# Gates and branch projections with weights 512 wide as the moving operand, merged branches transposed, weight loads held at the start

## The chip, the cores and the metric
One core of one Trainium2 chip. The metric is the device time of one execution, in microseconds (us).

## The reference
One layer of a hybrid encoder, 256 tokens by 2048 channels, float32. The parts that the change touches:

```
h = RMSNorm_pre(x)
gate_logits = (h @ W_in)[..., last 4096 columns]
g_ssm, g_attn = split(sigmoid(gate_logits + b_gate))        # 2 x (256, 2048)
merged = g_ssm * (y_ssm @ W_ssm_out) + g_attn * (y_attn @ W_attn_out)
x = x + RMSNorm_post(merged @ W_mix_out)
```

y_ssm has 4096 channels and y_attn 2048. Before this come the other columns of W_in, the state-space scan and the attention; behind it a feed-forward block (up projection, convolution, GeGLU, down projection).

## The kernel before
Every product with a weight is made in three parts, so that it is nearly exact in float32: ACT copies a weight slot to a rounded high part w_hi (`split`, L480), DVE takes raw minus w_hi as the low part w_lo (`lo`, L824), and the activations lie in SBUF as a high and a low part side by side. hi x hi, hi x lo and lo x hi are added up in PSUM. The unit of this stream is a half: 128 x 512 weights, 256 KB. SP loads raw weights in units of two halves into four slots; there are four slots of w_hi and w_lo, and ACT and DVE run up to three halves ahead of TensorE (LEAD = 3).

There are two ways to use a half on TensorE (PE). `half` (L1345) is narrow: the weights are stationary, 128 columns at a time, and the activations move, 512 columns (high and low) against w_hi and 256 columns (high) against w_lo: eight matmuls, 3072 moving columns. The output is transposed, channels on partitions, 256 tokens in columns; the low columns and the high ones lie in two halves of a bank. ACT copies one of them to `tmp` (`main_copy`, L489) and DVE adds the other (`evac`, L830). `wide_half` (L1357) is the other way: 128 tokens of activations are stationary and the weights move, 512 columns, three matmuls for each of two groups of tokens: six matmuls, 3072 moving columns. The output has tokens on partitions and needs one read of a bank.

The stages are Q and S (the projections with attention and scan beside them), G (gates, 128 halves), O (branches, 192 halves), M (mix, 64 halves), U (up, 256 halves) and D (down, 128 halves). M and D are wide, the others narrow. Each engine has its own program in order, loops (`Fori`) with the same turn structure on all engines, and semaphores: `lo_done` (w_lo is there), `half_used` (PE is done with a half), `tile_out` (an output tile has been read from its banks). G beside its products makes the grouped RMSNorm of the scan's output: squares on ACT, their sums on GpSimd, a product with ones on PE behind a turn's seventh half (L1537), scaling and splitting into y_s on DVE and ACT. In O a turn makes 256 channels of both branches: 16 halves of y_s and 8 of o_s; DVE multiplies with the gate (`gated_branch`), adds the branches (`merge`), and the sum, already transposed, is split into h_s (`merged_hi` L689, `merged_lo` L1176) for M. Behind the last turn the merge and the split come before ACT loads its Sqrt table (L735) and before M's next splits; three halves of M have been split by then.

At the start SP issues two 1 MB loads of x and then the weight loads without a wait. DVE and ACT square each half of x as it lands, x is scaled, PE transposes it (`h_bank`, L1372), ACT and DVE split it into h_s, and the first halves go in between.

Of the kernel before, what the change touches and what calls it, by code (L numbers as in the profile page):

```python
# [24 lines left out]
F32 = mybir.dt.float32  # L25
# [39 lines left out]
for _name, _n in (("mix_pre", 16), ("ffn_pre", 16), ("gate_b", 32), ("xbc_b", 48), ("ssm_norm", 32),  # L65
                  ("ffn_b", 64), ("xbc_w", 192), ("ffn_w", 192)):
    PAR[_name] = _at
    _at += _n
# [7 lines left out]
for _name, _halves, _tiles in (("Q", 136, 34), ("S", 320, 80), ("G", 128, 32), ("O", 192, 32), ("M", 64, 8),  # L76
                               ("U", 256, 64), ("D", 128, 8)):
    HALF[_name], TILE[_name] = _h, _t
    _h += _halves
    _t += _tiles  # L80
HALVES = _h
LEAD = 3
# [4 lines left out]
PAR_LOADS = 12  # L87
# [32 lines left out]
def build(nc, x, norm_mix_pre, norm_mix_post, norm_ffn_pre, norm_ffn_post, w_in, b_gate, conv_xbc_w,  # L120
# [3 lines left out]
    with ctx:  # L124
# [9 lines left out]
        def place(name, shape, dt, at):  # L134
# [11 lines left out]
        w_lo, at = place("w_lo", [P, 4, 2, 256], F32R, at)  # L146
        tmp, at = place("tmp", [P, 2, T], F32, at)
# [6 lines left out]
        mt_b, _ = place("mt_b", [P, 2, 3 * P], F32, at)  # L154
        sq, at = place("sq", [P, 2, T], F32, at)
# [11 lines left out]
        gate, _ = place("gate", [P, 32, T], F32, RG)  # L167
# [90 lines left out]
        yn_done, yn_hi, y_split, gate_tanh, m_split = (sem(n) for n in (  # L258
            "yn_done", "yn_hi", "y_split", "gate_tanh", "m_split"))
# [30 lines left out]
        def _(sp):  # L290
# [37 lines left out]

            for m in range(4):
                plain(win, m, V0, m, m)  # L330
# [52 lines left out]
        def _(pool):  # L383
# [19 lines left out]
            rows = {"mix_pre": norm_mix_pre, "ffn_pre": norm_ffn_pre, "gate_b": b_gate, "xbc_b": conv_xbc_b,  # L403
# [54 lines left out]
            with pool.Fori(0, GROUPS) as i:  # L458
                for n in range(3):
# [15 lines left out]
        def _(act):  # L475
# [188 lines left out]
            with act.Fori(0, GROUPS) as i:  # L664
                for j in range(16):
# [23 lines left out]
            def merged_hi(i):  # L689

                for t in range(2):
                    act.wait_ge(yn_done, i * 2 + (33 + t))
                    dst = h_s[:, 2 * i + t, 0:T] if isinstance(i, int) else (
                        h_s[:, bass.ds(i * 2 + t, 1), 0:T].rearrange("p a t -> p (a t)"))
                    act.activation(dst, yn[:, t, :], ACT.Copy, scale=0.5).then_inc(yn_hi, 1)

            def branch_turn(i, before):
                for j in range(24):
                    split(i, 24, H + j + LEAD)
                    if before is not None and j == 3:  # L700
                        merged_hi(before)
                    if j in (2, 4, 6, 8):
                        g = i * 2 + ((j - 2) // 4 * 16 + (j - 2) // 2 % 2)
                        act.activation(tile_of(gate, g), tile_of(gate, g), ACT.Tanh, scale=0.5,
                                       bias=col("gate_b", g)).then_inc(gate_tanh, 1)
                    if j in (15, 23):
                        for t in range(2):
                            n = 2 * (j // 16) + t
                            main_copy(i, 24, 4, H + j, N + n, n)

            branch_turn(0, None)
            with act.Fori(1, 8) as i:
                branch_turn(i, i - 1)
            merged_hi(7)
# [909 lines left out]
```

## Time and profile before

| | us |
|---|---|
| median of 3 runs (lowest, highest) | 1855.43 (1854.22, 1856.04) |
| profiled execution | 1854.61 |
| its span, first to last instruction | 1852.8 |
| PE busy | 1809.3 (98%) |
| DVE busy | 1310.1 (71%) |
| ACT busy | 1113.7 (60%) |
| GpSimd busy | 95.5 (5%) |
| HBM read | 340.05 MB, with writes 185 GB/s |

The granted clock of TensorE is 0.993 as a mean. A busy PE is not PE at its peak: matmuls overlap, so the distance between starts tells the pace, not the duration of one. LDWEIGHTS (PEld) is the load of the stationary operand and overlaps the matmul before it.

### The profile page before, as it was taken

Reading aid. Unit: us, or ns where it says so; the run is one execution under the profiler, and the core shown is the slowest. Engines: PE = TensorE matmul, PEld = TensorE weight load, DVE = VectorE, ACT = ScalarE, POOL = GpSimd, SP = SyncE. Lnnn points to the kernel's source line nnn. Section 1 sums busy time; section 2 is a strip of 40 time slices with the busy share of each in tenths; the row PEclk is TensorE's granted clock in tenths of the full one; section 3 lists DMA queues with packets and bytes.
Section 4 is the critical chain, followed back from the end, with each engine's and each line's share of the span. In section 5 each row is a group of like instructions: output and inputs, shape, how many; then the busy total and the mean of one; then the engine's idle time right before and its main releaser. Section 6 shows DMA issues by size and latency. Waiting matters only on the chain.

```text
span 1852.8 us, 36223 instructions
## 1 busy us (share of the span) xinstructions
PE 1809.3 (98%) x10131; PEld 1556.3 (84%) x10131; DVE 1310.1 (71%) x2510; ACT 1113.7 (60%) x2223; POOL 95.5 (5%) x154
## 2 busy tenths in 40 slices
PE   7999999999999999999999999997999999999997
PEld 6888888888888888888888888886888888887886
DVE  5766688888888888777756655655677777775554
ACT  6554566666666666777655555545666666664443
POOL 2000001110010110111100000000000000000000
PEclk9999999999999999999999999999999999999999
DMA  7656656765666665566655555665466666665664
GB/s 205 201 163 189 181 178 176 204 188 166 201 188 181 175 203 168 172 183 186 185 190 179 188 190 183 205 225 183 137 191 183 192 191 192 185 181 182 193 196 144
DMA packets 402986, 342.80 MB, mean 185 GB/s; under 512 B 28960, under 2 KB 373168, under 8 KB 402432
## 3 DMA queue, kind: packets, MB, share of 16 engines
q1 hardware_dynamic: 398240, 325.14, 58.7%
q0 software_dynamic: 4672, 17.15, 2.8%
q8 instruction: 20, 0.33, 0.1%
q14 instruction: 22, 0.18, 0.0%
q10 hardware_dynamic: 32, 0.01, 0.0%
HBM read 340.05 MB, written 2.16 MB: 185 GB/s over the span
## 4 chain that ended last, share of the span: by engine, by line
PE 92%; DVE 3%; ACT 2%; issue 2%; DMA 0%; DVEq 0%; ACTq 0%; SPq 0%
PE bank L1351 49%; PE bank L1353 25%; PE bank L1364 14%; PE bank L1369 3%; ACT w_hi L487 1%; DVE cc L1016 1%; DMA x_rows<-in_x 0%; PE bank L1483 0%; DVE xc L1027 0%; ACT mix_junk L749 0%; DVE w_lo L827 0%; DVE out_t L1339 0%; DVE upad L833 0%; ACT cc L597 0%; PE bank L1383 0%
## 5 line engine op out<-in xcount | busy, mean ns | idle before, releaser
L827 DVE TENSOR_TENSOR w_lo<-raw,w_hi 128x512 fp32r<-128x512 f32 x1224 | 844.5, 697 | 447.6 <-ACT w_hi L487 433.1
L487 ACT ACTIVATE w_hi<-raw 128x512 fp32r<-128x512 f32 x1224 | 756.6, 628 | 444.6 <-PE bank L1353 318.8
L1351 PE MATMUL bank<-h_s,w_hi 128*128 128x512 f32 x2336 | 840.2, 403 | 0.4 <-DVE h_s L845 0.3
L1353 PE MATMUL bank<-h_s,w_lo 128*128 128x256 f32 x2336 | 655.2, 280 | 0.0
L1351 PEld LDWEIGHTS bank<-h_s,w_hi 128*128 128x128 f32 x2336 | 439.2, 188 | 108.7 <-issue 4.6
L1351 PE MATMUL bank<-o_s,w_hi 128*128 128x512 f32 x1280 | 446.8, 393 | 0.0
L1353 PEld LDWEIGHTS bank<-h_s,w_lo 128*128 128x128 f32 x2336 | 441.8, 189 | 0.6
L1353 PE MATMUL bank<-o_s,w_lo 128*128 128x256 f32 x1280 | 358.6, 280 | 0.0
L1351 PEld LDWEIGHTS bank<-o_s,w_hi 128*128 128x128 f32 x1280 | 239.7, 187 | 53.8
L1353 PEld LDWEIGHTS bank<-o_s,w_lo 128*128 128x128 f32 x1280 | 241.9, 189 | 0.0
L1351 PE MATMUL bank<-y_s,w_hi 128*128 128x512 f32 x512 | 181.2, 399 | 0.0
L1364 PE MATMUL bank<-w_hi,y_s 128*128 128x512 f32 x512 | 159.2, 392 | 3.1 <-DVE w_lo L827 3.1
L1353 PE MATMUL bank<-y_s,w_lo 128*128 128x256 f32 x512 | 143.8, 281 | 0.0
L494 ACT ACTIVATE tmp<-bank 128x256 f32<-128x256 f32 x242 | 79.7, 382 | 101.1 <-PE bank L1353 101.1
L1364 PEld LDWEIGHTS bank<-w_hi,y_s 128*128 128x128 f32 x512 | 96.8, 189 | 23.7 <-DVE w_lo L827 3.5
L1351 PEld LDWEIGHTS bank<-y_s,w_hi 128*128 128x128 f32 x512 | 96.2, 188 | 24.1
L1364 PE MATMUL bank<-w_lo,y_s 128*128 128x512 f32 x256 | 100.3, 392 | 0.0
L1353 PEld LDWEIGHTS bank<-y_s,w_lo 128*128 128x128 f32 x512 | 96.7, 189 | 0.0
L1364 PE MATMUL bank<-w_hi,h_s 128*128 128x512 f32 x256 | 80.5, 394 | 2.1 <-DVE w_lo L827 2.1
L1364 PEld LDWEIGHTS bank<-w_hi,h_s 128*128 128x128 f32 x256 | 48.9, 191 | 12.9 <-DVE w_lo L827 2.6
L1016 DVE SCALAR_TENSOR_TENSOR cc<-upad,par,cc 128x256 f32<-128x256 f32 x144 | 59.0, 479 | 0.0
L1364 PEld LDWEIGHTS bank<-w_lo,y_s 128*128 128x128 f32 x256 | 48.5, 189 | 10.1
(205 smaller groups left out, 1191.4 us busy)
## 6 DMA issues: line engine op xcount, KB each, us to landing
raw<-in_w_in SPq DMA_DIRECT2D x576, 256.0 KB, 3.0
raw<-in_w_up SPq DMA_DIRECT2D x256, 256.0 KB, 3.2
raw<-in_w_ssm_out SPq DMA_DIRECT2D x128, 256.0 KB, 2.9
raw<-in_w_down SPq DMA_DIRECT2D x128, 256.0 KB, 3.4
raw<-in_w_attn_out SPq DMA_DIRECT2D x64, 256.0 KB, 2.9
raw<-in_w_mix_out SPq DMA_DIRECT2D x64, 256.0 KB, 3.6
cs_rows<-cs_dram POOLq DMA_DIRECT2D x16, 512.0 KB, 4.9
cs_rows<-cs_dram POOLq DMA_DIRECT2D x16, 256.0 KB, 6.2
```

What stands on the lines that cost most here:

```text
L487: act.activation(w_hi[:, c % 4, :, :], raw[:, slot, 2 * m:2 * m + 2, :], ACT.Copy).then_inc(hi_done, 1)
L494: act.activation(tmp[:, n % 2, :], bank[b][:, 0:T], ACT.Copy).then_inc(main_out, 1)
L827: dve.tensor_tensor(w_lo[:, c % 4, :, :], raw[:, (c // 2) % 4, 2 * (c % 2):2 * (c % 2) + 2, :], w_hi[:, c % 4, :, :].bitcast(F32), ALU.sub ...
L1016: ins = dve.scalar_tensor_tensor(out=cc[:, t, :], in0=upad[:, t, n:n + T], scalar=col("xbc_w", tile[t] + n * 48), in1=cc[:, t, :], op0=ALU ...
L1351: pe.matmul(bank[b][:], w_hi[:, w[0], w[1], w[2]], src[:, k0 + k, :], start=start and k == 0, stop=False, skip_group_check=True)
L1353: last = pe.matmul(bank[b][:, T:2 * T], w_lo[:, w[0], w[1], w[2]], src[:, k0 + k, 0:T], start=False, stop=True, skip_group_check=True)
L1364: last = pe.matmul(bank[b + t][:], src[:, kt, at + P * t:at + P * t + P], w, start=kt == 0 and w is hi and at == 0, stop=True, skip_group_ ...
L1369: return pe.matmul(o, a, b, start=start, stop=True, skip_group_check=True)
```

## The change
G and O use `wide_half`. In G a turn makes 1024 gate columns in two groups of sixteen halves; the gates lie with tokens on partitions, and DVE adds the bias, which GpSimd loads for each 512 columns and spreads to all partitions (`gate_out`); ACT's copies and the bias in ACT's tanh are gone. In O there are four turns of 48 halves instead of eight of 24; DVE multiplies straight from the bank, 512 columns by 128 tokens at a time, and adds the branches into a new tile `both`. The sum now has tokens on partitions, so PE transposes it, eight 128 x 128 transposes for each 512 channels (`merged_t`), behind the sixth half of the next turn, the last ones behind M's third half; ACT and DVE split the result from PSUM, likewise later in the turn. ACT waits for all gates before its first tanh. SP's loads for G and O are `wide`: rows of 2 KB instead of 1 KB. At the start SP waits for the first half of x before the first weight load, and PE makes six products of ones and the identity once x's second half is there. `UNCOPIED` only shifts counts.

```diff
@@ sync
+            sp.wait_ge(x_in[0], 16)
             for m in range(4):
                 plain(win, m, V0, m, m)
...
-            with sp.Fori(0, 16) as i:
-                for m in range(4):
-                    plain(win, m, i * 256 + GATE0, i * 4 + (u + m), m)
+            with sp.Fori(0, GROUPS) as i:
+                for m in range(8):
+                    wide(win, m, i * WIDE + GATE0, i * 8 + (u + m), m % 4)
             u = HALF["O"] // 2
-            with sp.Fori(0, 8) as i:
+            with sp.Fori(0, 4) as i:
+                for m in range(16):
+                    wide(wssm, m, i * WIDE, i * 24 + (u + m), m % 4)
                 for m in range(8):
-                    plain(wssm, m, i * 256, i * 12 + (u + m), m % 4)
-                for m in range(4):
-                    plain(wattn, m, i * 256, i * 12 + (u + 8 + m), m)
+                    wide(wattn, m, i * WIDE, i * 24 + (u + 16 + m), m % 4)
@@ gpsimd, G
             with pool.Fori(0, GROUPS) as i:
+                pool.wait_ge(tile_out, i * 2 + TILE["G"])
+                pool.dma_start(gate_bias[:], b_gate[:, bass.ds(i * WIDE, WIDE)].rearrange("a c -> (a c)")
+                               .partition_broadcast(P)).then_inc(bias_in, 16)
@@ scalar, G, O and M
-                    if j % 8 == 7:
-                        for t in range(2):
-                            k = j // 8
-                            main_copy(i, 16, 4, H + j, N + 2 * k + t, 2 * k + t)
...
+            def merged_hi(c):
+                for n in range(4):
+                    kt = c * 4 + n
+                    act.wait_ge(m_mm, c * 4 + (n + 1))
...
+                    act.activation(dst, bank[4 + n][:, 0:T], ACT.Copy, scale=0.5).then_inc(m_hi, 1)
             def branch_turn(i, before):
-                for j in range(24):
-                    split(i, 24, H + j + LEAD)
-                    if before is not None and j == 3:
+                for j in range(48):
+                    split(i, 48, H + j + LEAD)
+                    if before is not None and j == 7:
                         merged_hi(before)
                     if j in (2, 4, 6, 8):
...
+                        at = gate[:, t, bass.ds(i * WIDE + D * b, WIDE)]
+                        act.activation(at, at, ACT.Tanh, scale=0.5).then_inc(gate_tanh, 1)
+            act.wait_ge(tile_out, N)
...
+            def mix_turn(i, first):
                 for k in range(2):
                     for j in range(16):
                         split(i, 32, H + 16 * k + j + LEAD)
+                        if first and (k, j) == (0, 1):
+                            merged_hi(3)
@@ vector, G and O
+            def gate_out(i, k):
+                dve.wait_ge(half_used, i * 32 + (H + 16 * k + 16))
+                dve.wait_ge(bias_in, i * 32 + (16 * k + 16))
+                for t in range(2):
+                    dve.tensor_tensor(gate[:, t, bass.ds(i * (2 * WIDE) + WIDE * k, WIDE)], bank[2 * k + t][:], gate_bias[:],
+                                      ALU.add).then_inc(tile_out, 1)
...
             def gated_branch(i, b):
+                dve.wait_ge(half_used, i * 48 + (H + 32 + 16 * b))
                 for t in range(2):
+                    g = gate[:, t, bass.ds(i * WIDE + D * b, WIDE)]
+                    dve.wait_ge(gate_tanh, i * 4 + (2 * b + t + 1))
+                    dve.scalar_tensor_tensor(out=g, in0=g, scalar=1.0, in1=bank[2 * b + t][:], op0=ALU.add,
+                                             op1=ALU.mult).then_inc(tile_out, 1)
             def merge(i):
                 for t in range(2):
+                    dve.wait_ge(tile_out, i * 4 + (N + 3 + t))
+                    dve.tensor_tensor(both[:, t, :], gate[:, t, bass.ds(i * WIDE, WIDE)],
+                                      gate[:, t, bass.ds(i * WIDE + D, WIDE)], ALU.add).then_inc(merged, 1)
+            def merged_lo(c):
+                for n in range(4):
...
+                    dve.wait_ge(m_hi, c * 4 + (n + 1))
+                    dve.scalar_tensor_tensor(out=part(T), in0=bank[4 + n][:, 0:T], scalar=0.5, in1=part(0).bitcast(F32),
+                                             op0=ALU.mult, op1=ALU.subtract).then_inc(m_split, 1)
+            def branch_turn(i, before):
+                for j in range(48):
+                    lo(i, 48, H + j + LEAD)
+                    if before is not None and j == 7:
+                        merged_lo(before)
+                    if j in (31, 47):
+                        gated_branch(i, j // 47)
+                merge(i)
@@ tensor
+            pe.wait_ge(x_in[1], 16)
+            for n in range(6):
+                mm(bank[3][:, 0:P], ones[:], ident[:])
             for kt in range(4):
                 h_bank(kt)
...
+                    for j in range(16):
+                        wide_half(i, 32, H + 16 * k + j, h_s, j, 2 * k)
+                        if j == 6:
+                            pe.wait_ge(sq_added, i * 6 + (3 * k + 3))
+                            pe.wait_ge(misc_read, i * 2 + (MISC_G + k))
+                            mm(misc[:, 0:T], ones[:], sq_sum[:]).then_inc(misc_ready, 1)
...
+            def merged_t(c):
+                pe.wait_ge(merged, c * 2 + 2)
+                for n in range(4):
+                    for t in range(2):
+                        last = pe.transpose(bank[4 + n][:, P * t:P * t + P], both[:, t, P * n:P * n + P], ident[:])
+                    last.then_inc(m_mm, 1)
+            def branch_turn(i, before):
+                pe.wait_ge(tile_out, i * 4 + (N - 2))
+                for j in range(32):
+                    pe.wait_ge(y_split, j + 1)
+                    wide_half(i, 48, H + j, y_s, j, 0)
+                    if before is not None and j == 5:
+                        merged_t(before)
+                pe.wait_ge(tile_out, i * 4 + N)
+                for j in range(16):
+                    wide_half(i, 48, H + 32 + j, o_s, j, 2)
...
+            def mix_turn(i, first):
                 for k in range(2):
                     pe.wait_ge(tile_out, i * 4 + (N + 2 * k - 2))
                     for j in range(16):
-                        if k == 0:
+                        if first and k == 0:
                             pe.wait_ge(m_split, j + 1)
                         wide_half(i, 32, H + 16 * k + j, h_s, j, 2 * k)
+                        if first and (k, j) == (0, 2):
+                            merged_t(3)
```

## Rows read from the trace of the kernel before

**Rows 1.** The page: busy time of an engine; the chain that ended last.

```profile
PE 1809.3 (98%) x10131; PEld 1556.3 (84%) x10131; DVE 1310.1 (71%) x2510; ACT 1113.7 (60%) x2223; POOL 95.5 (5%) x154
...
PE 92%; DVE 3%; ACT 2%; issue 2%; DMA 0%; DVEq 0%; ACTq 0%; SPq 0%
```

**Rows 2.** In order of time, PE, end of O and M: start, duration, [idle before].

```profile
1190.02 0.40 PE L1351 MATMUL bank<-o_s,w_hi 128*128 128x512 f32 x1
...
1194.62 0.40 PE L1351 MATMUL bank<-o_s,w_hi 128*128 128x512 f32 x1
...
1194.97 0.40 PE L1364 MATMUL bank<-w_hi,h_s 128*128 128x512 f32 x1
...
1196.13 0.62 PE L1364 MATMUL bank<-w_hi,h_s 128*128 128x512 f32 x2
...
1198.17 0.62 PE L1364 MATMUL bank<-w_hi,h_s 128*128 128x512 f32 x2
...
1201.38 0.50 PE L1364 MATMUL bank<-w_hi,h_s 128*128 128x512 f32 x1 [2.15 <-DVE w_lo L827]
```

**Rows 3.** Busy time by stretch; the sixth entry is the granted clock.

```profile
1202.00:1206.00 4.00, 4.00 (x12) 3.13 (x11) 1.83 (x3) 0.80 (x2) 0.00 (x0) 0.57 1.01 417
```

**Rows 4.** In order of time, PE, the first turn of G.

```profile
745.18 0.50 PE L1351 MATMUL bank<-h_s,w_hi 128*128 128x512 f32 x1 [0.15 <-DVE w_lo L827]
...
750.72 0.28 PE L1353 MATMUL bank<-h_s,w_lo 128*128 128x256 f32 x1
...
751.50 0.28 PE L1353 MATMUL bank<-h_s,w_lo 128*128 128x256 f32 x1
```

**Rows 5.** In order of time, PE: first product of O, last of M.

```profile
923.61 0.40 PE L1351 MATMUL bank<-y_s,w_hi 128*128 128x512 f32 x1
...
1285.89 0.39 PE L1364 MATMUL bank<-w_hi,h_s 128*128 128x512 f32 x1
```

**Rows 6.** In order of time, PE, the start of D.

```profile
1662.34 0.62 PE L1364 MATMUL bank<-w_hi,y_s 128*128 128x512 f32 x2
...
1665.78 0.39 PE L1364 MATMUL bank<-w_hi,y_s 128*128 128x512 f32 x1
```

**Rows 7.** In order of time, PE: low products around four transposes at the start.

```profile
19.95 0.28 PE L1353 MATMUL bank<-h_s,w_lo 128*128 128x256 f32 x1
...
20.73 0.28 PE L1353 MATMUL bank<-h_s,w_lo 128*128 128x256 f32 x1
```

**Rows 8.** Groups of instructions: busy us, mean ns of one, idle before.

```profile
L827 DVE TENSOR_TENSOR w_lo<-raw,w_hi 128x512 fp32r<-128x512 f32 x1224 | 844.5, 697 | 447.6 <-ACT w_hi L487 433.1
...
L487 ACT ACTIVATE w_hi<-raw 128x512 fp32r<-128x512 f32 x1224 | 756.6, 628 | 444.6 <-PE bank L1353 318.8 <-PE bank L1364 120.4 <-DMA raw<-in_w_mix_out 3.1
...
L1223 DVE TENSOR_TENSOR gained<-bank,mix_gain 128x512 f32 x8 | 5.5, 692 | 4.5 <-ACT mix_junk L726 4.0
```

**Rows 9.** In order of time: a bank of M is handed over.

```profile
1220.84 0.39 PE L1364 MATMUL bank<-w_hi,h_s 128*128 128x512 f32 x1
...
1221.19 0.60 ACT L726 ACTIVATE mix_junk<-bank 128x512 f32<-128x512 f32 x1 [0.89 <-PE bank L1364]
```

**Rows 10.** In order of time, the start.

```profile
10.62 1.23 DVE L853 CUSTOM_DVE_ANT_0 junk<-x_rows 128x1024 f32<-128x1024 f32 x1 [1.38 <-DMA x_rows<-in_x]
...
13.43 1.97 PE L1383 MATMUL bank<-ident,x_rows 128*128 128x128 f32 x8 [9.70 <-ACT x_rows L500]
...
15.66 0.80 PE L1351 MATMUL bank<-h_s,w_hi 128*128 128x512 f32 x1 [0.26 <-DVE h_s L845]
...
18.57 0.49 PE L1351 MATMUL bank<-h_s,w_hi 128*128 128x512 f32 x1
```

**Rows 11.** Busy time by stretch, the start; the last entry is GB/s.

```profile
0.00:10.00 10.00, 0.26 (x1) 0.18 (x1) 1.23 (x2) 2.70 (x5) 1.85 (x12) 1.00 0.78 241
...
8.00:10.00 2.00, 0.00 (x0) 0.00 (x0) 1.23 (x2) 1.22 (x3) 0.00 (x0) 1.00 1.02 394
10.00:12.00 2.00, 0.00 (x0) 0.00 (x0) 1.30 (x3) 1.15 (x2) 0.00 (x0) 1.00 1.10 360
```

More of the change, by code:

```diff
@@ L154, in build @@
         mt_b, _ = place("mt_b", [P, 2, 3 * P], F32, at)
+        both, _ = place("both", [P, 2, WIDE], F32, at)
         sq, at = place("sq", [P, 2, T], F32, at)
@@ L166, in build @@
         out_t, _ = place("out_t", [P, 2, D], F32, RO)
-        gate, _ = place("gate", [P, 32, T], F32, RG)
+        gate, _ = place("gate", [P, 2, 2 * D], F32, RG)
         gained, _ = place("gained", [P, 2, D], F32, RG)
@@ L697, in branch_turn @@
             def branch_turn(i, before):
-                for j in range(24):
-                    split(i, 24, H + j + LEAD)
-                    if before is not None and j == 3:
+                for j in range(48):
+                    split(i, 48, H + j + LEAD)
+                    if before is not None and j == 7:
                         merged_hi(before)
                     if j in (2, 4, 6, 8):
[L703 to L709, printed above, removed]
+                        t, b = (j // 2 - 1) % 2, (j - 2) // 4
+                        at = gate[:, t, bass.ds(i * WIDE + D * b, WIDE)]
+                        act.activation(at, at, ACT.Tanh, scale=0.5).then_inc(gate_tanh, 1)
@@ L1238, in _ @@
                         lo(i, 32, H + 16 * k + j + LEAD)
-                    if k == 0:
+                        if first and (k, j) == (0, 1):
+                            merged_lo(3)
+                    if first and k == 0:
                         dve.wait_ge(gain_in[0], 16)
                     wide_gain(i, 4, N + 2 * k, 2 * k, mix_gain, k)
-            inverse(0, lambda: dve.wait_ge(main_out, N + 8))
+            mix_turn(0, True)
+            with dve.Fori(1, 2) as i:
+                mix_turn(i, False)
+            inverse(0, lambda: dve.wait_ge(main_out, N - UNCOPIED + 8))
             dve.wait_ge(x_again_in, 32)
@@ L1531, in _ @@
             H, N = HALF["G"], TILE["G"]
[L1532 to L1555 removed]
+            with pe.Fori(0, GROUPS // 2) as i:
                 for k in range(2):
@@ L1558, in _, with mix_turn @@
                     for j in range(16):
-                        if k == 0:
+                        wide_half(i, 32, H + 16 * k + j, h_s, j, 2 * k)
[3 more added lines that the diff above has]
+                            mm(misc[:, 0:T], ones[:], sq_sum[:]).then_inc(misc_ready, 1)
+            H, N = HALF["O"], TILE["O"]
+            def merged_t(c):
[14 more added lines that the diff above has]
+                    wide_half(i, 48, H + 32 + j, o_s, j, 2)
+            branch_turn(0, None)
+            with pe.Fori(1, 4) as i:
+                branch_turn(i, i - 1)
+            H, N = HALF["M"], TILE["M"]
+            def mix_turn(i, first):
+                for k in range(2):
+                    pe.wait_ge(tile_out, i * 4 + (N + 2 * k - 2))
+                    for j in range(16):
+                        if first and k == 0:
                             pe.wait_ge(m_split, j + 1)
                         wide_half(i, 32, H + 16 * k + j, h_s, j, 2 * k)
+                        if first and (k, j) == (0, 2):
+                            merged_t(3)
+            mix_turn(0, True)
+            with pe.Fori(1, 2) as i:
+                mix_turn(i, False)
             def h2_bank(kt):
```

149 lines of the change are left out of this document (46 added, 103 removed).

## The prediction
> **What bounds the kernel now.** I read the page's busy shares and its chain of waits first, then TensorE in order of time at the edges of the stages the change touches. TensorE (PE) is busy 98% of the span and holds 92% of the chain [rows 1]; ACT and DVE have room. So time is what the PE stream costs per half (one slot of split weights, 3072 moving columns either way), plus what the PE loses at stage edges and at the start. The reader is to see three things.
>
> First, the pace. A narrow half is four pairs of 512 and 256 columns. Late in the branch stage, 13 pairs take 1194.62 - 1190.02 = 4.60 us, 0.354 a pair, 1.41 us a half. A wide half is two triples of 512 columns: three triples take 1198.17 - 1196.13 = 2.04 us, 0.680 a triple, 1.36 us a half [rows 2]. The columns are equal (1.28 us at 2.4 GHz); what differs is the eight instructions against six.
>
> Second, one edge: entering the mix stage the PE stands 2.15 us for a w_lo [rows 2], and right behind it four microseconds have a mean clock of 0.57, so PE is at 1.2 GHz most of that time: 4 x 0.43 = 1.7 us more [rows 3].
>
> Third, the start: the PE's first transpose is at 13.43, 2.81 us after the second half of x lets DVE go at 10.62 [rows 10].
>
> **Gates (128 halves).** Seven halves precede the row-sum product. Halves 3 to 6 start at 745.18, after a stall of 0.31 (0.15 of it shown as idle), and three halves at 1.41 lie before it, so the stage starts at 745.18 - 0.31 - 4.23 = 740.64 [rows 4]. The branch stage starts at 923.61 [rows 5]: 182.97 us. The row-sum product of ones moves the low product from 750.72 to 751.50, 0.78 where a pair takes 0.35: 0.43 us, eight times 3.44 [rows 4]. That and the 0.31 stay. After: 128 x 1.36 + 3.44 + 0.31 = 177.8. **Saved 5.1.**
>
> The PSUM traffic changes hands: ACT's copies go, DVE adds a bias to two 512-wide banks per sixteen halves, 0.69 us each [rows 8]. PE uses the other pair of banks for the next 16 halves (22 us), so this costs nothing. DVE's burst of 1.5 us delays the next w_lo; PE has three halves (4.08 us) in hand. On GpSimd the bias DMA and its wait (the last tile's eviction) come before the row-sum adds; they start about 2.5 us later in a group, and their product is wanted only after seven halves, 9.5 us: hidden. SP issues as many transfers of the same size. At the end ACT waits for DVE's last bias additions, with its splits behind it: 0.35 + 1.5 us, then split 0.63 and w_lo 0.70 [rows 8, 9] gives 3.2 of the 4.08 us: hidden, 0.9 us in hand, and lost one for one beyond.
>
> **Branches (192 halves).** Before: 1194.97 - 923.61 = 271.36 us [rows 2, 5], 1.413 a half throughout. After: 192 x 1.36 = 261.1. Added: eight transposes per chunk, three chunks here. Four of the start's transposes move the low product by 20.73 - 19.95 - 0.35 = 0.43 us [rows 7], so eight take 0.85: 2.55 in all. PE's new y_split waits are met long before. The end of each turn is the tight place. DVE gets the bank about 0.35 us after the next half has begun (1220.84 against 1221.19, where ACT is the reader [rows 9]); two gate products and two merges of 512 columns at 0.69 with a 0.06 gap make 3.0 (fused products are not shown at this width; as bounds I take the 0.69 and 0.70 of the plain ones, 0.75 if their scalar form costs more); then w_lo 0.70. That is 4.05 against 4.08 us of PE work. The weight load of that half wants to go first, so I take 0.2 us of stall at each of three turns (0 to 0.5): 0.6. At the gate products of the first branch the burst is only 1.5 us: nothing. ACT's four tanh of a turn, 512 wide, and its four halved copies (about 1.6 us in a row) come when it has seven or more halves before the next edge; it needs 0.63 of 1.36 us: hidden. After: 264.3. **Saved 7.1.**
>
> **Mix.** Before: from 1194.97 to 1285.89 + 0.23 = 1286.12 [rows 2, 5], 91.15 us, which is 64 x 1.36 = 87.04 and 4.1 of loss (stall 2.4, clock 1.7). The stall was DVE's and ACT's last merge, then the Sqrt table, then split and w_lo, one after the other. After, ACT loads the table and goes on splitting; the merge's copies wait until the transposes behind the third half. What is late next is w_lo of half 3 (the same 4.05 against 4.08: 0.2) and, behind four copies and four splits, w_lo of half 5 (0.15). Transposes 0.85. The 3 MB that GpSimd asks for at this edge now meet a PE that is 4 us ahead; weights of halves 10 and 11 are issued 3 us earlier too, so I take nothing, with 2 us as the bad bound. After: 88.2. **Saved 2.9** (0 to 3.8).
>
> **Start.** Weights wait for the first half of x. By 10.6 us the queues moved 2.41 MB + 0.6 x 0.36 = 2.6 MB, of which x is 2.1: half a megabyte of weights went between, 1.3 us at 0.39 MB/us [rows 11]. I take 1.2 (0 to 1.4). Held weights are issued at about 7 to 8 us and the first slot, at most 1 MB with what is left of x, takes 2.6 us; it is wanted past 12: hidden. Below nothing it could go only by that slot being late, at most 1 us. The six added products lie in the 2.8 us between x's landing and the first transpose: by the 0.43 us of a 256-column product at full clock, 128 columns at half clock cost 0.43, six 2.6. Then first half and four transposes, 18.57 - 15.66 = 2.91 us before [rows 10], take 1.41 + 0.43 if the clock is up: 1.07 less, of which I take 0.7, since the second half also waits for h. **Saved 1.9** (-1 to 2.4).
>
> On that clock: before, PE began with transposes at 13.43 and ordinary products at 15.66, and rows behind 18 have full-clock durations [rows 10]. The Trainium skill ("TensorE: Matmul & The Clock Gate", Part 4: PE-mode transpose) says that transposes do not count as PE activity for the clock. By that rule the added products are the only activity before the first half, and the 0.7 may be absent, since PE then only transposes for 2 us; the trace cannot separate the two readings.
>
> **Sum.** 5.1 + 7.1 + 2.9 + 1.9 = 17.0 us off the profiled execution's 1854.61 us (its span 1852.8 and 1.8 around it): 1837.6. The median of the runs shown is 1855.43, 0.8 above it; I forecast 1838.0.
>
> **Rivals.**
> (a) Wide halves in these stages run as at the start of the down projection: 1665.78 - 1662.34 = 3.44 us for five triples, 0.688 [rows 6], 1.376 a half. 320 x 0.016 = 5.1 back; and with nothing from the start, 1.9 more. 1843 to 1845. For: narrow halves pace differently by stage too. Against: mix holds 0.680.
> (b) The gain per half is not there: only columns count, and the fewer instructions bring nothing. Then the transposes (2.55) and turn stalls (0.6) stand against mix and start (4.8): 1.65 us saved, 1853. Against: 1.41 and 1.36 stand on the two sides of one edge, 2 us apart [rows 2]. The Trainium skill ("TensorE: Matmul & The Clock Gate", Back-to-back issue gap) puts the gap of a full-clock matmul at N/2.4 + 2.5 ns. By it a narrow half is 1.300 and a wide one 1.295, an estimate of 320 x 0.005 = 1.6 us in all, so 1851.7 here. The rows have 0.227 for 512 columns, 13 ns above the columns, not 2.5; the measurement decides.
> (c) Slower: the handover in the branches. If DVE's burst at the eight handovers of that stage, from the bank's release to w_lo, is 2.1 us longer than 4.05, PE stalls as at the old mix edge, and the clock drops each time: 4.1 x 8 = 33 us, 1870. It turns the sign when each costs more than 2.1 us. For: the margin at the four turn ends is nil. Against: the mid-turn handovers have 1.5 us of slack, and the durations are well known.
> (d) Better: no turn stalls, the full start gain and 3.8 at mix: 1835 or a little less.
>
> **How the numbers follow.** Forecast and its neighbourhood with (d), 1833 to 1841: 0.70. (a), 1841 to 1846: 0.18. Between (a) and (b): 0.05. (b): 0.03. (c): 0.04. The range, 1832 to 1846, holds the first two and leaves out under 2 in 10. A measurement of this kernel tells 0.2%, 3.7 us, from no change, so faster is all but (b) and (c): 0.93; same is (b), 0.03; slower (c), 0.04.
>
> **What would show it.** The wide products of the gate and branch stages at 0.680 a triple, about 178 and 264 us between the first products of the stages; no idle PE at the mix edge and a clock of 1.0 there; turn ends with at most 0.3 us of idle before a wide product, released by w_lo; eight transposes in 0.85 us; DVE's first look at x's second half near 9.4 and the first half's products at full-clock durations from its first pair. Wrong would be: 0.688 or more a triple, idle of 1 us or more at turn ends, ACT waiting for raw weights at the start or past the mix edge, or products of 0.43 us spacing there.

## The result and the profile after

| | us |
|---|---|
| changed kernel, median of 6 runs | 1846.39 (1839.73 to 1849.49) |
| kernel before beside it, 6 runs | 1855.74 (1854.22 to 1861.21) |
| ratio | 0.9939, 95% interval 0.9921 to 0.9956 |
| profiled execution of the changed kernel: its span | 1844.3 |

The forecast was 1838.0 with a range of 1832 to 1846: faster as forecast, but by 9.3 us instead of 17.4, and the median is 0.4 above the upper end of the range. The page answers to [rows 1]:

```profile
PE 1804.5 (98%) x9535; PEld 1529.3 (83%) x9535; DVE 1288.5 (70%) x2437; ACT 1096.2 (59%) x2143; POOL 99.8 (5%) x161
...
PE 91%; DVE 3%; ACT 2%; issue 2%; DMA 1%; DVEq 0%; ACTq 0%; SPq 0%
```

PE still sets the time. It has some 600 instructions fewer, as eight products a half became six in 320 halves (640 fewer), while 32 transposes and the six products (two rows each) were added: 10131 - 9535 = 596. Its busy time fell by only 4.8. So the stages have to be read one by one. Their edges are the first products of G, O and M, the last of M, and the first of D (start, duration):

```profile
740.41 0.40 PE L1371 MATMUL bank<-w_hi,h_s 128*128 128x512 f32 x1
...
919.01 0.39 PE L1371 MATMUL bank<-w_hi,y_s 128*128 128x512 f32 x1
...
1182.85 0.39 PE L1371 MATMUL bank<-w_hi,h_s 128*128 128x512 f32 x1
...
1272.24 0.39 PE L1371 MATMUL bank<-w_hi,h_s 128*128 128x512 f32 x1
...
1655.11 0.40 PE L1371 MATMUL bank<-w_hi,y_s 128*128 128x512 f32 x1
```

The same edges, taken in the profile of every kernel that is told of below, in us. "To G" is the time from the start of the span. G of "before" and of e10 begins at the point worked out as in the prediction, G of e2 and e5 at the 512th product with w_hi ahead of O. "M to U" is the gap between M's last product and the first of U's opening; D ends with its last product, and about 11.7 us follow it in every profile.

| profile | to G | G | O | M | M to U | U | D | span |
|---|---|---|---|---|---|---|---|---|
| before | 740.64 | 182.97 | 271.36 | 91.15 | 11.83 | 363.93 | 179.13 | 1852.8 |
| after | 740.41 | 178.60 | 263.84 | 89.62 | 11.46 | **371.18** | 177.51 | 1844.3 |
| e1, after again | 739.77 | 178.58 | 263.84 | 90.60 | 11.46 | 363.71 | 179.11 | 1838.7 |
| e5, before again | 741.55 | 182.84 | 266.23 | 91.14 | 11.84 | 371.72 | 180.17 | 1857.2 |
| e2, narrow G and O | 740.24 | 183.16 | 271.26 | 90.01 | 11.46 | 363.79 | 179.10 | 1850.8 |
| e3, no hold | 740.14 | 178.62 | 263.84 | 92.48 | 11.45 | 363.99 | 179.11 | 1841.3 |
| e4, no six products | 741.67 | 178.57 | 263.84 | 93.68 | 11.45 | 363.75 | 179.08 | 1843.7 |
| e6, late x | 740.28 | 178.57 | 263.84 | 87.95 | 11.45 | 363.78 | 179.11 | 1836.7 |
| e7, products in U | 740.59 | 178.58 | 263.84 | 90.57 | 11.45 | 374.36 | 180.32 | 1851.4 |
| e8, other order | 734.64 | 178.57 | 263.84 | 92.12 | 11.46 | 365.47 | 180.25 | 1838.1 |
| e9, other order, late x | 734.58 | 178.57 | 263.84 | 87.95 | 11.46 | 366.83 | 179.11 | 1834.0 |
| e10, before in the other order | 735.87 | 182.28 | 267.52 | 91.17 | 11.83 | 365.62 | 180.29 | 1846.2 |

The first two lines say where the gain went. G gave 4.37, O 7.52, M 1.53, D 1.62 (behind D's opening stall of 3.1 us the products kept their full pace; in every other profile some of them run at half pace, so this is luck and no part of the change), the start 0.23, the gap before U 0.37: 15.6 us. U, whose code is the same in both kernels, took 7.25 back, and 15.6 - 7.25 = 8.4 is what the spans differ by, within 0.1.

What PE waited for in the changed kernel (total us, times, longest):

```profile
PE bank L1376 <- DVE diag L1259: 11.3, 1, 11.3
PE bank L1376 <- DMA x_rows<-in_x: 6.7, 1, 6.7
PE bank L1371 <- DVE w_lo L835: 4.7, 3, 3.1
PE bank L1395 <- DMA mix_rows<-in_norm_mix_pre: 3.6, 1, 3.6
PE bank L1493 <- DVE o_s L1013: 1.1, 7, 0.2
PE bank L1358 <- DVE h_s L853: 0.3, 1, 0.3
```

Only three waits are for w_lo: 3.1 where D begins, 1.40 in M, and 0.25 in G's third half, the one that [rows 4] have. None of the handovers of a bank in G and O stalls, neither at turn ends nor inside them. In O, the chunk's eight transposes between two wide products, in order of time:

```profile
992.22 0.39 PE L1371 MATMUL bank<-w_hi,y_s 128*128 128x512 f32 x1
992.46 1.03 PE L1560 MATMUL bank<-ident,both 128*128 128x128 f32 x8
993.25 0.48 PE L1371 MATMUL bank<-w_hi,y_s 128*128 128x512 f32 x1
993.56 0.39 PE L1371 MATMUL bank<-w_lo,y_s 128*128 128x512 f32 x1
...
994.25 0.40 PE L1371 MATMUL bank<-w_lo,y_s 128*128 128x512 f32 x1
...
994.94 0.39 PE L1371 MATMUL bank<-w_lo,y_s 128*128 128x512 f32 x1
...
995.62 0.39 PE L1371 MATMUL bank<-w_lo,y_s 128*128 128x512 f32 x1
```

The transposes hold the next product back by 993.25 - 992.46 = 0.79, and the one behind it comes after 0.31 instead of 0.227, 0.09 more. Read the low products behind them: 0.69, 0.69, 0.68 apart. Whatever is put between wide products leaves the next few triples 0.01 longer; then they are at 0.680 again.

The edge into M, which answers to [rows 2, 3], on ACT, DVE, GpSimd (POOL) and PE:

```profile
1182.34 1.28 ACT L736 ACT_TABLE_LOAD   x1
...
1183.25 1.28 DVE L1183 SCALAR_TENSOR_TENSOR gate<-gate,bank 128x512 f32 x2 [0.20 <-PE bank L1371]
1183.31 1.07 POOL L476 DMA_DIRECT2D x_again<-in_x  x2 [280.29 <-PE bank L1371]
...
1184.45 1.29 DVE L1189 TENSOR_TENSOR both<-gate 128x512 f32 x2
...
1197.42 1.15 ACT L495 ACTIVATE w_hi<-raw 128x512 fp32r<-128x512 f32 x2 [4.67 <-DMA raw<-in_w_mix_out]
...
1198.92 0.47 PE L1371 MATMUL bank<-w_hi,h_s 128*128 128x512 f32 x1 [1.40 <-DVE w_lo L835]
```

The old stall of 2.15 is gone: ACT has the table at 1183.6 and goes on splitting. DVE's burst lasts from 1183.25 to 1184.45 + 1.29 = 1185.74, 2.49 us and not the 3.0 of the forecast, since two products of 512 columns take 1.28 and not 1.44. But some 15 us into M a new stall stands: ACT has no raw weights for 4.67 us, and PE runs dry for 1.40. Two megabytes of x, asked for by GpSimd at 1183.31, are the suspect; e6 below moves them. Windows of after, then of e6, in which the two loads of x come later (the third figure from the end is the granted clock, then DMA share and GB/s):

```profile
1190.00:1195.00 5.00, 5.00 (x24) 4.14 (x23) 2.39 (x4) 1.38 (x3) 0.00 (x0) 1.00 0.96 340
```

```profile
1190.00:1195.00 5.00, 5.00 (x24) 4.14 (x23) 2.92 (x5) 2.23 (x4) 0.00 (x0) 1.00 0.79 247
```

At the start, against [rows 10]:

```profile
10.61 1.23 DVE L861 CUSTOM_DVE_ANT_0 junk<-x_rows 128x1024 f32<-128x1024 f32 x1 [1.38 <-DMA x_rows<-in_x]
10.63 2.93 PE L1376 MATMUL bank<-ident,ones 128*128 128x128 f32 x12 [6.73 <-DMA x_rows<-in_x]
...
13.42 1.97 PE L1390 MATMUL bank<-ident,x_rows 128*128 128x128 f32 x8
15.65 0.50 PE L1358 MATMUL bank<-h_s,w_hi 128*128 128x512 f32 x1 [0.26 <-DVE h_s L853]
...
17.84 0.50 PE L1358 MATMUL bank<-h_s,w_hi 128*128 128x512 f32 x1
```

(The six products appear as x12, two rows each.) The second half of x comes at 10.61 where it came at 10.62: the hold brought nothing. The first half of the stream begins at the same 15.65, but its first product takes 0.50 and not 0.80, and the second half begins at 17.84 where it began at 18.57: 0.73 less.

The U stage: low products of after, fifteen pairs from the first row to the last:

```profile
1399.88 0.28 PE L1360 MATMUL bank<-o_s,w_lo 128*128 128x256 f32 x1
...
1405.18 0.28 PE L1360 MATMUL bank<-o_s,w_lo 128*128 128x256 f32 x1
```

and of e1, the same kernel run again:

```profile
1399.97 0.28 PE L1360 MATMUL bank<-o_s,w_lo 128*128 128x256 f32 x1
...
1405.17 0.28 PE L1360 MATMUL bank<-o_s,w_lo 128*128 128x256 f32 x1
```

5.30 / 15 = 0.3533 a pair against 5.20 / 15 = 0.3467. U has 1024 pairs, and 1024 x 0.0067 = 6.8 us of the 7.5 between the two profiles. The narrow stream has two paces.

### The profile page after: what moved, and what is told of

The parts are those of the page before. It is cut to its first block, busy times and chain, and to the rows that moved or that the text cites. A ratio compares the mean times of both kernels' runs of the same rounds, so it can differ in the third digit from the quotient of the medians.

```text
span 1844.3 us, 34324 instructions
## 1 busy us (share of the span) xinstructions
PE 1804.5 (98%) x9535; PEld 1529.3 (83%) x9535; DVE 1288.5 (70%) x2437; ACT 1096.2 (59%) x2143; POOL 99.8 (5%) x161
## 4 chain that ended last, share of the span: by engine, by line
PE 91%; DVE 3%; ACT 2%; issue 2%; DMA 1%; DVEq 0%; ACTq 0%; SPq 0%
PE bank L1371 37%; PE bank L1358 33%; PE bank L1360 17%; PE bank L1376 3%; ACT w_hi L495 1%; DVE cc L1024 1%; DMA raw<-in_w_mix_out 1%; DMA x_rows<-in_x 0%; PE bank L1493 0%; DVE w_lo L835 0%; DVE xc L1035 0%; ACT mix_junk L757 0%; DVE upad L841 0%; DVE out_t L1346 0%; ACT cc L605 0%
## 5 line engine op out<-in xcount | busy, mean ns | idle before, releaser
L1358 PE MATMUL bank<-h_s,w_hi 128*128 128x512 f32 x1824 | 658.4, 403 | 0.4 <-DVE h_s L853 0.3
L1360 PE MATMUL bank<-h_s,w_lo 128*128 128x256 f32 x1824 | 512.0, 281 | 0.0
L1358 PEld LDWEIGHTS bank<-h_s,w_hi 128*128 128x128 f32 x1824 | 342.6, 188 | 85.9 <-issue 4.7
L1360 PEld LDWEIGHTS bank<-h_s,w_lo 128*128 128x128 f32 x1824 | 344.8, 189 | 0.4
L1371 PE MATMUL bank<-w_hi,y_s 128*128 128x512 f32 x1024 | 317.0, 389 | 3.1 <-DVE w_lo L835 3.1
L1371 PE MATMUL bank<-w_hi,h_s 128*128 128x512 f32 x768 | 240.8, 392 | 1.7 <-DVE w_lo L835 1.7
L1371 PEld LDWEIGHTS bank<-w_hi,y_s 128*128 128x128 f32 x1024 | 192.2, 188 | 43.4 <-DVE w_lo L835 3.5
L1371 PE MATMUL bank<-w_lo,y_s 128*128 128x512 f32 x512 | 199.2, 389 | 0.0
L1371 PEld LDWEIGHTS bank<-w_hi,h_s 128*128 128x128 f32 x768 | 144.1, 188 | 32.5 <-issue 1.8
L1371 PE MATMUL bank<-w_lo,h_s 128*128 128x512 f32 x384 | 149.4, 389 | 0.0
```

The lines of the kernel that those rows point to most:

```text
L1358: pe.matmul(bank[b][:], w_hi[:, w[0], w[1], w[2]], src[:, k0 + k, :], start=start and k == 0, stop=False, skip_group_check=True)
L1360: last = pe.matmul(bank[b][:, T:2 * T], w_lo[:, w[0], w[1], w[2]], src[:, k0 + k, 0:T], start=False, stop=True, skip_group_check=True)
L1371: last = pe.matmul(bank[b + t][:], src[:, kt, at + P * t:at + P * t + P], w, start=kt == 0 and w is hi and at == 0, stop=True, skip_group_ ...
```

## The experiments

**e1: the changed kernel, unchanged.** No edit; it asks what the program's own runs do.

> The changed kernel as it is, to see how the same program varies. In the profile of the change the up projection, whose code is unchanged, runs at 0.353 us per narrow pair from its second turn to its end (371.2 us from first product to the down projection's first); before it ran at 0.347 (363.9 us). Theory A: a stream of narrow pairs is locked in one of two paces and keeps it until something else is put in between, which pace it gets is chance, and this is what hides 7 us of the gain. Then single runs spread over about 7 to 10 us (1839 to 1850), and this profile's up projection takes either 364 or 371 us, with the profiled time following: about 1839 to 1841 with 364, 1846 to 1848 with 371. Theory B: the change itself slows the up projection (data placement, what is left in flight). Then it is at 0.353 in every profile of a kernel with the change, and the spread of the runs has another place.

Measured: 1842.91 us (median of 12, 1840.4 to 1851.44), the kernel before beside it 1850.16 (18 runs, 1847.45 to 1857.34), ratio 0.9966 (0.9949 to 0.9983). The times lie in groups: seven between 1840.4 and 1843.2, five between 1846.7 and 1851.5. Those of before do too: twelve at 1847.5 to 1850.4, six at 1855.6 to 1857.4. One program therefore has steps of about 7 us in it, as large as the effect that was to be measured: beside this set the change is worth 7.3 us, beside the first one 9.3. The table shows what one such step is: U at 363.71 in place of 371.18; G and O agree within 0.02. Even its faster group is 2 to 5 us above the forecast of 1838.

**e5: the kernel before, once more, profiled.**

> The kernel before once more, for its stages in a second profile. Theory A (paces by chance): its branch stage, 271.36 us at 0.353 a pair in the first profile, takes 266.3 or 271.4 us, the gates again alternate between 0.347 and 0.353 from turn to turn, and the up projection takes about 364 or 371 us; the runs of the kernel before fall in groups some 7 us apart accordingly (1848 to 1850 and 1856 to 1857 beside the last set). If the branch stage is 266.3 here, the change's gain in it is 2.5 us and not 7.5. Theory B (paces belong to the code): the same three numbers as in the first profile, 271.4 and 363.9.

Measured: 1859.21. Its O takes 266.23 where it took 271.36, its U 371.72 where it took 363.93. The low products of its O, fifteen pairs:

```profile
999.85 0.28 PE L1353 MATMUL bank<-y_s,w_lo 128*128 128x256 f32 x1
...
1005.05 0.27 PE L1353 MATMUL bank<-y_s,w_lo 128*128 128x256 f32 x1
```

0.3467, where [rows 2] have 0.354. So the 1.41 us a half on which the forecast rests is not a property of the narrow form, but one of its two paces. G again has both: from one row-sum product to the next its pace is 0.353, twice 0.347, then 0.353 and 0.347 by turns.

**e2: G and O narrow again, all else as changed.**

```diff
-                        wide_half(i, 32, H + 16 * k + j, h_s, j, 2 * k)
+                        half(i, 32, H + 16 * k + j, h_s, 2 * (j % 8), 2 * k, 2 * k + 1, j == 0)
...
-                    wide_half(i, 48, H + j, y_s, j, 0)
+                    half(i, 48, H + j, y_s, 2 * (j % 16), 0, 1, j == 0)
...
-                    wide_half(i, 48, H + 32 + j, o_s, j, 2)
+                    half(i, 48, H + 32 + j, o_s, 2 * (j % 8), 2, 3, j == 0)
```

One line more is changed: O's first half waits for all of y_s at once, and the other halves no longer wait for it.

> The changed kernel with TensorE's products in the gate and branch stages narrow again (weights stationary, 512 and 256 moving columns), all else as changed: loads, bias additions, gate products, transposes, edges. The sums in the banks then are not the reference's; only the time counts. Theory A (the gain in the two stages is the pace of the stream, 1.36 us a half against 1.387 or 1.413): the 320 halves take 320 x 0.027 to 0.053 = 8.6 to 17 us more, 1855 to 1863 us by the median, and the two stages show 0.347 or 0.353 a pair. Theory C (the gain comes from what stands around the products, ACT's copies and the edges, and the stream's form is worth 0.005 a half): within 2 us of the change.

Measured: 1860.25 (7 runs, 1852.44 to 1862.85), ratio to before 1.0041 (1.002 to 1.0062), where the changed kernel beside it had 0.9966. All else that was changed, taken together (the transposes, DVE's and ACT's new work, the start), does not make the kernel faster; the gain hangs on the wide products. The profiled execution is the fastest of the seven: its span is 1850.8 against e1's 1838.7, 12.1 more, of which G has 4.6 and O 7.4 (271.26 against 263.84), with U alike (363.79, 363.71). In its G the pace switches at each row-sum product, 0.3467 and 0.3533 by turns, as it does in the kernel before from its second one on. In its O it switches at each of the three groups of transposes, so O here is half at either pace.

**e7: a product of ones inside each of U's turns.** From its second turn on U has nothing between its narrow products that could switch the pace; here one product is put in.

```diff
                         half(i, 16, H + 8 * k + j, o_s, 2 * j, 2 * k, 2 * k + 1, j == 0)
+                        if not first and (k, j) == (0, 6):
+                            mm(misc[:, 0:T], ones[:], par[:, 0:T])
```

> The changed kernel with one product of ones and 256 columns of constants, as in the gates stage before, put into each turn of the up projection behind its seventh half; its result is not used. In the gates stage before, the pace changed at each such product and held in between. Theory A (the pace is a locked state that an inserted product switches): the up projection shows 0.347 and 0.353 in turn, takes (364 + 371)/2 + 15 x 0.43 = 374 us whatever the start, and the runs lie close together, near 1849. Theory H (the pace belongs to the turn's data or to the time of the other engines): one pace throughout, 370 or 377 us, and the spread of 7 us stays.

Measured: U 374.36, kernel 1851.86 (12 runs, 1848.96 to 1853.74). Low products of two turns that follow each other, eleven pairs each:

```profile
1327.47 0.28 PE L1360 MATMUL bank<-o_s,w_lo 128*128 128x256 f32 x1
...
1331.29 0.28 PE L1360 MATMUL bank<-o_s,w_lo 128*128 128x256 f32 x1
...
1350.10 0.28 PE L1360 MATMUL bank<-o_s,w_lo 128*128 128x256 f32 x1
...
1353.99 0.28 PE L1360 MATMUL bank<-o_s,w_lo 128*128 128x256 f32 x1
```

3.82 / 11 = 0.347, then 3.89 / 11 = 0.354, and from there each stretch is at the other pace than the one before it. Of the fifteen products put in, the first left the pace as it was and the other fourteen each switched it; between two of them it never changed. The spread is 4.8 us instead of 11, as one expects when each execution has both paces in U in about equal parts. So the pace holds until something comes between. That U's pace is what divides e1's groups fits the two profiles at hand (U 371.18 at 1845.96 us, 363.71 at 1840.40); the other runs have no profile.

**e8: another order in the narrow form.** High, high, low, low instead of high, low, high, low.

```diff
                     for t, b in enumerate((b0, b1)):
                         pe.matmul(bank[b][:], w_hi[...], src[:, k0 + k, :], ...)
+                    for t, b in enumerate((b0, b1)):
                         last = pe.matmul(bank[b][:, T:2 * T], w_lo[...], src[:, k0 + k, 0:T], ...)
```

> The changed kernel with the products of every narrow half in another order: for each of the two rows of weights first both 512-column products, then both 256-column ones (instead of 512, 256, 512, 256). The work and the sums are the same. Theory J (the two paces come from the phase of the stream as a whole): 0.347 and 0.353 as averages per pair remain, and the median is within 1 us of the change.

Measured: 1839.81 (6 runs, 1836.88 to 1840.32), ratio 0.992 (0.9896 to 0.9944). U's low products now come in pairs; two pairs apart:

```profile
1399.95 0.39 PE L1360 MATMUL bank<-o_s,w_lo 128*128 128x256 f32 x2
...
1404.83 0.40 PE L1360 MATMUL bank<-o_s,w_lo 128*128 128x256 f32 x2
```

seven times two pairs in 4.88, 0.349 a pair; over 800 pairs of U it is 0.3483, between the two old paces, and the same in e9 and e10. U takes 365.47, near the fast one. So the two paces belong to the order of the products, and not to the stream whatever its order (theory J); whether the weight load is the reason, as theory I has it, no run shows. The time up to G is 5.8 us less than in after and 5.1 less than in e1: the narrow stream of Q and S has two paces as well, and in after its stretches are at the slow one about five times as often as at the fast one. The spread is 3.4 us.

**e10: the kernel before with e8's order**, so that change and no change can be compared without the two paces.

> The kernel before with its narrow products in the order high, high, low, low, and nothing else: all its narrow stages then run at one pace, as those of the changed kernel with the same order do (1839.8). Theory (the change is worth about 5 us at like pace: G 320 pairs... worked out as 128 and 192 halves of 1.39 us against 1.36 plus eight transposes per chunk, start 0.7, M 1 us worse): about 1844.5 here, G near 181.5 and O near 267. Rival 1 (the whole gain of the change was the pace that the narrow stream happened to take): 1840 or less, the same as the changed kernel with this order. Rival 2 (the change is worth the 9 us that were measured, whatever the order): 1849.

Measured: 1847.51 (12 runs, 1844.18 to 1849.02); e8 is 1839.81, and the profiled spans are 8.2 apart. The two ran on different chips, but e9, on e10's chip, has e8's 178.57 for G and 263.84 for O, so the stages can be compared. That is nearer to the second rival (1849) than to the 1844.5 of the theory, which had G at 181.5 (182.28 measured), O at 267 (267.52) and M 1 us worse (0.95). It missed most in G (0.8), in O and at the start (0.5 each). The rival that the gain was all pace (1840) is out. Stage by stage e10 minus e8: 1.23 + 3.71 + 3.68 - 0.95 + 0.37 + 0.15 + 0.04 = 8.2 us (to G, G, O, M, the gap, U, D). M is where the changed kernel loses, although e10 keeps the old stall:

```profile
1192.10 0.50 PE L1364 MATMUL bank<-w_hi,h_s 128*128 128x512 f32 x1 [2.16 <-DVE w_lo L827]
```

**e6: x_again later.** The two loads of x wait for halves 14 and 32 of M.

```diff
-            for s in range(2):
-                pool.dma_start(x_again[:, s, :], x_view[:, s, :]).then_inc(x_again_in, 16)
             pool.dma_start(mix_gain[:], ...)
+            for s in range(2):
+                pool.wait_ge(half_used, HALF["M"] + 14 + 18 * s)
+                pool.dma_start(x_again[:, s, :], x_view[:, s, :]).then_inc(x_again_in, 16)
```

> The changed kernel with GpSimd's two loads of x for the residual (2 MB) put behind half 14 and half 32 of the mix stage, and only the 1 MB of gains at its start. Theory F (3 MB asked for at the mix edge make the weights of halves 10 and 11 late, now that the edge itself does not stall: ACT waited 4.9 to 7.1 us for raw weights and the PE 1.4 to 3.9, and the clock fell behind the longer ones): the mix stage takes 88 us instead of 89.6 to 93.7, ACT's wait for raw goes, and the median falls by 2 to 4 us. Theory G (the wait is the order of SyncE's own loads behind the late w_lo of halves 3 to 5): the PE still stands 1 us or more at about half 10.

Measured: 1838.75 (6 runs, 1838.37 to 1844.68), ratio 0.9931 (0.9905 to 0.9957). M is 87.95, which is 64 x 1.36 = 87.04 and the 0.9 of the transposes: no stall is left, and the gap before U is unchanged. The window shown above has 247 GB/s and ACT busy 2.23 us, where after had 340 and 1.38. So the loads of x held up the weights; the 1 MB of gains, still asked for at the edge, did not. The loads of x cost M 1.7 to 5.7 us in the other profiles of the changed kernel, a different amount each time; where the stall was longest (e4), it was 3.8 us and the clock fell behind it, 0.81 as a mean from 1198 to 1207.

**e3: without the hold at the start.**

```diff
-            sp.wait_ge(x_in[0], 16)
```

> The changed kernel with SyncE's wait for x's first half taken out ahead of the weight loads. Theory D (the hold brings nothing: the second half of x landed at 10.6 us before as after, since its bytes go ahead of the weights on the same queue): DVE's look at the second half stays at 10.6 us, and the first product at 15.65. Theory E (weights take bandwidth from x, and something else kept the second half late in the changed kernel): it moves later by 0.5 us or more, to above 11.1.

Measured: 1843.0 in the one run. The second half of x:

```profile
10.63 1.22 DVE L860 CUSTOM_DVE_ANT_0 junk<-x_rows 128x1024 f32<-128x1024 f32 x1 [1.40 <-DMA x_rows<-in_x]
```

10.63 with the weights free, 10.61 with them held. The weights are issued on the same SP queue behind x. From 8 to 10 us 394 GB/s are moved here and 324 with the hold, and x lands at the same time: what the weights moved, x did not lose. It is one run of each, but before and after say the same.

**e4: without the six products** (and their wait).

```diff
-            pe.wait_ge(x_in[1], 16)
-            for n in range(6):
-                mm(bank[3][:, 0:P], ones[:], ident[:])
```

> The changed kernel with the six products of ones and their wait taken out. If they bring TensorE's clock up earlier: the first half's products run at 1.2 GHz again (its first pair apart by 0.6 us instead of 0.33), and the second half starts at 18.57 instead of 17.84 us, 0.7 later. If the clock rises by the transposes alone, or the hold did it: 17.84 stays.

Measured: 1845.36 in the one run. The first products of the stream and the first of the second half:

```profile
13.31 1.97 PE L1390 MATMUL bank<-ident,x_rows 128*128 128x128 f32 x8 [9.28 <-ACT x_rows L508]
15.54 0.80 PE L1358 MATMUL bank<-h_s,w_hi 128*128 128x512 f32 x1 [0.26 <-DVE h_s L853]
...
16.34 0.63 PE L1358 MATMUL bank<-h_s,w_hi 128*128 128x512 f32 x1
...
16.99 0.63 PE L1358 MATMUL bank<-h_s,w_hi 128*128 128x512 f32 x1
...
18.97 0.54 PE L1358 MATMUL bank<-h_s,w_hi 128*128 128x512 f32 x1
```

A pair takes 0.65 up to 18, as before the change. That is the pace of half clock: e9 has 0.64 a pair at the beginning of U, at a granted clock of 0.50. (The row of the granted clock itself says 1.00 here, from 15.50 to 18.20; at the start it does not show what the products do.) The second half begins 1.13 later than in after, and G 1.26 later. The six products do bring the full pace forward. Transposes that began at 13.31 had not brought it by 15.54; products that began at 10.63 had, by 15.65. That agrees with the Trainium skill ("TensorE: Matmul & The Clock Gate", Part 4: PE-mode transpose), which says that a transpose does not count as PE-busy in the same way. The reservation is that the products also began 2.7 us earlier, and this is one run. What the prediction feared from that rule, that the gain of 0.7 would be absent, did not happen.

**e9: e8 and e6 together.**

> The changed kernel with both edits at once: narrow products in the order high, high, low, low, and the reload of x delayed to M's turns. If the two act on different stages they add: the order alone gave 1839.8 with M at 92.1 us; the delay brings M to 88.0, so 1839.8 - 4.1 = 1835.7, with the start to G at 734.6, U at 365.5 and a spread of 2 us or less outside of single runs, since the narrow stream then has one pace. Rival: the delayed transfers of x fall on U's start, where the narrow stream now takes weights at the same rate as before, and M to U grows from 11.5 by 1 to 3 us: 1837 to 1839.

Measured: 1835.36 (6 runs, 1832.69 to 1835.7), ratio 0.9886 (0.9862 to 0.9909). The two add up as expected, 1835.7. The gap before U is the same 11.46; the rival has no case. U is 1.4 longer than in e8, 1.2 of it in its first eight products: 2.70 us at a granted clock of 0.50, where e8's take 1.48; why the clock came up later is open. This is the fastest version, faster than both kernels.

## Why the prediction came out as it did

- **G, 5.1 saved: 4.4 in the profiles, size off by 0.8.** A triple has its 0.680, and no wait appeared; G is 178.6, not 177.8. G has 4.5 us over its 128 x 1.36 where 3.75 was taken: 0.44 for each of eight row-sum products (0.43 taken), 0.5 for the stall in the third half (0.31 taken), and 0.5 in steps of a hundredth, as shown behind the transposes.
- **O, 7.1 saved: 7.5 against the profile of before, 2.4 against the same kernel's other profile (266.23).** The wide side was right: 263.84 for 264.3. O has 2.72 over 192 x 1.36, so a group of transposes costs 0.9 for the assumed 0.85. The stall at turn ends did not come; DVE's burst is 2.5 and not 3.0, which leaves half a microsecond where none was.
- **M, 2.9 saved: 1.5, 0.6 in e1.** The old stall went as forecast, and with it the fall of the clock. The step that failed is the one on the 3 MB that GpSimd asks for at this edge, "so I take nothing, with 2 us as the bad bound": it cost 1.7 in after and 2.7 in e1 (M less e6's 87.95), and more in others. e6 shows the cause; with x out of the way M is 87.95, as good as the 88.2 of the forecast.
- **Start, 1.9: 0.7.** The clock term was right (0.73). The term of the hold, 1.2, was wrong: half a megabyte of weights had moved beside x, but x was none the later for it. I had read a rate as if all of it were x's to have; e3 shows that it was not. At G the start is 0.2 ahead in after and 0.9 in e1; the two paces of the stream in Q and S stand between, so these two figures do not measure the start.
- **The covers** (bias on GpSimd, DVE's additions, ACT's tanh, y_split, weights at the start) all held: the list of PE's waits has none of them.
- **The step that failed most is one that I did not write down**: that code that is not changed keeps its time. U gave 7.25 us back in the profiled execution, on a pace that changes by chance from one execution to another. [Rows 2] showed 0.354, and rival (a) even says that narrow halves "pace differently by stage too"; I took it as against the wide form and did not ask what would happen if a stage came out at its other pace. The trace of before had O at 0.353 and U at 0.347: 5.1 us of O's cost hung on one pace, and 7.5 us of U's on the other.
- **The rivals.** (a) 0.688 in place of 0.680: no, only for a few triples behind something interposed. (b) No gain per half: no, 3.7 us in G and 3.7 in O even against the middle pace. The gap of N/2.4 + 2.5 ns, which the Trainium skill gives for an isolated full-clock matmul ("TensorE: Matmul & The Clock Gate", Back-to-back issue gap), does not hold for this stream, a case that the prediction did not tell apart: 13 ns over the columns for 512 (0.680 / 3 = 0.2267 against 0.2133), and (346.7 - 320) / 2 = 13 for the products of the fast narrow pair. (c) Slower handovers: none stalled. (d) Better: of its three parts only the missing stall at turn ends came.

The like-paced comparison, e10 against e8, gives the change 7.7 us in the medians and 8.2 in the spans; the two comparisons of the kernels as they are gave 9.3 and 7.3. From the forecast's 17.0 to 8.2, by those two profiles: the narrow side was taken from an execution in which it was slow (O 271.36 for 267.52, G 182.97 for 182.28), 4.5; M at 92.12 for 88.2, and the old M there 0.02 longer, 3.9; the start 1.23 for 1.9, 0.7; the wide side of G 0.8 worse and that of O 0.5 better; the gap before U and the rest gave 0.6. 17.0 - 4.5 - 3.9 - 0.7 - 0.8 + 0.5 + 0.6 = 8.2. The mechanism was right; the sizes of the narrow side, of M and of the start were not, and how near the median came to the range is in part luck. The upper end of the range asks for 1855.43 - 1846 = 9.4 us, more than the 8.2 at like pace; the kernel before was taken in an execution with a slow O, and the median of the changed kernel is a mixture of its groups (1846.39 in the first six runs, 1842.91 in the twelve of e1).

## What to carry to other kernels

Before a duration per unit is used in a sum, take it from several places and executions: where two values a fixed step apart occur, the unit has two paces, and a change of a few us is hidden unless both kernels are run many times or an order of instructions is found that has one pace. Where PE gets ahead at a stage edge, list every transfer that is issued there, and put those that are not needed soon behind a count of later work. Before a hold is given a gain, check that what it holds back takes time from what stands ahead of it; here the weights behind x on one queue took none.

## What the runs showed of the hardware

- A stream of alternating 512 and 256 column products with a weight load each runs at 0.3467 or 0.3533 us a pair, and keeps the one it has as long as nothing comes between (960 pairs, U from its second turn on, in after, e1, before and e5). One product between them (fourteen of fifteen times in e7), or eight transposes (three of three in e2), switches it. Why there are two is open. The order high, high, low, low has 0.3483 in U of e8, e9 and e10 and in O of e10.
- Three products of 512 columns take 0.680 in every wide stage that was read, at full clock, and return to it within a few triples after a disturbance.
- Behind the stall of 3.1 us at D's start the clock falls in all other profiles (D 179.1 to 180.3) but not in after (177.5); what tells them apart is open.
